# Ranking 32 experts by their number of rows and letting the ten smallest share TensorE in pairs

## The reference, cut to what matters

```python
gsel = jnp.argmax(lg, axis=-1)
le_sel = jnp.take_along_axis(le, gsel[:, None, None], axis=1)[:, 0]
top_p, top_i = lax.top_k(jax.nn.softmax(le_sel, axis=-1), TOP_K_INNER)
eid = gsel[:, None] * EXPERTS_PER_GROUP + top_i
hg = silu(einsum('nd,edf->nef', x, ewg)) * einsum('nd,edf->nef', x, ewu)
y = y + einsum('nef,efd->nd', hg * gate[:, sl, None], ewd)
```

## Time and profile before

| what | value |
|---|---|
| median of 3 runs | 1778.75 us (1776.92 to 1789.27) |
| the profiled execution | 1779.9 us |
| its span | 1778.1 us |
| TensorE busy | 1628.3 us (92%) |
| VectorE, ScalarE, GpSimd busy | 672.5, 434.6, 55.5 us |
| mean granted TensorE clock | 0.953 |
| moved by DMA | 246.90 MB |

### The profile page before, as it was taken

How to read it: one execution, slowest core, us unless ns; L and a number is a source line. 1 busy time by engine, 2 the same in 40 slices (tenths; PEclk the granted TensorE clock), 3 DMA queues, 4 the chain that set the end, 5 groups by cost and what they waited for, 6 DMA issues and landing times. The chain is left out here.

```text
span 1778.1 us, 34951 instructions
## 1 busy us (share of the span) xinstructions
PE 1628.3 (92%) x15296; PEld 1144.4 (64%) x15296; DVE 672.5 (38%) x1631; ACT 434.6 (24%) x891; POOL 55.5 (3%) x57
## 2 busy tenths in 40 slices
PE   7899989989988889998989879999999999995997
PEld 4566775775676656675757654555788888883443
DVE  5365464464364213415151442234411111112564
ACT  4413314214202202304131231112111111111344
POOL 0000000000000000000000000000100000002110
PEclk9898999998997889999999989999999999997999
DMA  5000001000010043403242472004799999976321
GB/s 183 27 27 12 15 17 38 13 16 13 15 41 20 3 195 129 169 27 155 119 179 119 186 276 97 36 36 158 273 368 368 366 371 368 365 297 221 111 83 42
DMA packets 57597, 246.90 MB, mean 139 GB/s; under 512 B 7520, under 2 KB 18016, under 8 KB 47712
## 3 DMA queue, kind: packets, MB, share of 16 engines
q1 hardware_dynamic: 45632, 201.61, 30.3%
q0 software_dynamic: 7200, 26.22, 4.1%
q10 hardware_dynamic: 4608, 16.78, 2.3%
HBM read 210.70 MB, written 33.88 MB: 138 GB/s over the span
## 5 line engine op out<-in xcount | busy, mean ns | idle before, releaser
L438 PE MATMUL bank<-h,w 128*128 128x352 f32 (+1 forms) x576 | 198.6, 495 | 6.4 <-DVE xb L997 6.4
L1750 PEld LDWEIGHTS bank<-cache,we 128*128 128x128 f32 x1536 | 175.1, 192 | 13.7 <-issue 10.5
L1750 PE MATMUL bank<-cache,we 128*128 128x128 f32 x1536 | 175.6, 275 | 2.8 <-DVE cache L2019 2.8
L438 PEld LDWEIGHTS bank<-h,w 128*128 128x128 f32 x576 | 109.7, 198 | 69.6 <-DVE xb L997 7.6
L2019 DVE COPY cache<-bank 128x512 f32<-128x512 f32 x64 | 41.3, 686 | 289.3 <-PE bank L1737 289.3
L1241 PE MATMUL bank<-h,w 128*128 128x352 f32 (+1 forms) x384 | 120.8, 477 | 5.5 <-POOL qd L1226 5.5
L1681 PE MATMUL bank<-cache,mixed 128*128 128x512 f32 x256 | 113.0, 600 | 6.4 <-DMA mixed<-in_pad_a 6.4
L2286 PE MATMUL bank<-we,unT 128*128 128x512 f32 x256 | 114.2, 604 | 1.4 <-DVE unT L2237 1.4
L1241 PEld LDWEIGHTS bank<-h,w 128*128 128x128 f32 x384 | 74.2, 194 | 50.4 <-POOL qd L1226 6.1
L1681 PEld LDWEIGHTS bank<-cache,mixed 128*128 128x128 f32 x256 | 48.7, 193 | 65.5 <-issue 58.9
L2286 PEld LDWEIGHTS bank<-we,unT 128*128 128x128 f32 x256 | 48.9, 194 | 60.4 <-issue 58.6
(11 more groups left out here) (405 smaller groups left out, 2499.2 us busy)
## 6 DMA issues: line engine op xcount, KB each, us to landing
we<-in_weg SPq DMA_DIRECT2D x24, 1024.0 KB, 5.3
we<-in_weu SPq DMA_DIRECT2D x24, 1024.0 KB, 8.6
we<-in_wed SPq DMA_DIRECT2D x24, 1024.0 KB, 11.2
cache<-in_kcj SPq DMA_DIRECT2D x4, 5120.0 KB, 15.7
cache<-in_vcj SPq DMA_DIRECT2D x4, 5120.0 KB, 15.1
y_rows<-cache ACTq DMA_DIRECT2D x32, 512.0 KB
cache<-in_weg SPq DMA_DIRECT2D x8, 1024.0 KB
cache<-in_weu SPq DMA_DIRECT2D x8, 1024.0 KB
```

What stands on the lines that cost most here:

```text
L438: mm = pe.matmul(out[:, 0:w], w3[:, KIND[q], kd, :], g.uT[:, kd, a:a + w], start=(kd == 0), stop=(kd == KD - 1))
L1750: mm = pe.matmul(bank[6 + e % 2][:, 128 * (2 * a + f):128 * (2 * a + f) + CAP], w[:, k, 128 * f:128 * f + 128], xT[e % 2][:, k, :], start= ...
```

## The change

Places stand for experts. VectorE ranks the experts by their count, largest first, with experts 0 to 3 fixed in ranks 0 to 3. Ranks 0 to 9 have room for 128 rows, 10 to 21 for 96, 22 to 31 for 64 (`CAPS`). The table of tokens is reordered by rank into `idx`, and `order` holds the expert of each rank; SyncE reads it into a register and loads the weights from there (`load_chosen`). The 32 ranks make 27 turns (`TURNS`): ranks 0 and 1 singly, and then five times four single ranks and one pair of the last ten: 2 to 5, (22, 23), 6 to 9, (24, 25), and so on to 18 to 21, (30, 31). Loads follow the order of the turns through the same four slots; a load waits for the `down` of the turn that had its slot.

In a pair, each expert has 64 rows. Both are gathered into one buffer and turned at once. In `up` the 64 columns of `xT` are the stationary side and 256 columns of the weights move, each expert in its half of the array; the result has rows by hidden columns, so after SiLU and product two transposes (`hidden_turn`) turn it for `down`, which again uses both halves. Rows are stored densely, 3072 in all. `rows` is split in `first_rows` (after turns 1 and 2) and `later_rows` (after turns 3 and 4), with each expert's own room and start. The later passes run if any expert has more rows than its rank has room for.

```diff
+CAPS = [128] * 10 + [96] * 12 + [64] * 10
+BASE = [sum(CAPS[:e]) for e in range(NE)]
+SINGLES, PAIRED = CAPS.index(64), list(range(CAPS.index(64), NE, 2))
+TURNS = [(e,) for e in range(SINGLES - 4 * len(PAIRED))]
+for n, e in enumerate(PAIRED):
+    TURNS += [(len(TURNS) - n + i,) for i in range(4)] + [(e, e + 1)]
+NU = len(TURNS)
+IN_TURN = [e for places in TURNS for e in places]
+load_of = {e: n for n, e in enumerate(IN_TURN)}
+turn_of = lambda e: next(u for u, places in enumerate(TURNS) if e in places)
+rows_in = lambda u: sum(CAPS[e] for e in TURNS[u])
+pairs_to = lambda u: sum(len(places) == 2 for places in TURNS[:u + 1])
+gathers_to = lambda u: sum(len(TURNS[n]) for n in range(u % NX, u + 1, NX))
...
+def load_chosen(sp, g, slot, e, loaded):
+    wg, wu, wd = slot
+    at = bass.ds(e, 1)
+    sp.dma_start(wg, g.d_weg[at].rearrange("o (p k) f -> p (o k) f", p=128)).then_inc(loaded, 16)
+    sp.dma_start(wu, g.d_weu[at].rearrange("o (p k) f -> p (o k) f", p=128)).then_inc(loaded, 16)
+    sp.dma_start(wd, g.d_wed[at].rearrange("o (f p) d -> p (o f) d", p=128)).then_inc(loaded, 16)
...
-        LOADS = ((gain, g.d_ffn_gain), (wr, g.d_wr), (br, g.d_br), (upper, g.d_upper), (iota, g.d_iota), (valid[:, :], g.d_valid),
-                 (w4, g.d_w4), (w32, g.d_w32), (tokv[:, :], g.d_tokv), (i32t, g.d_i32t), (pad_a, g.d_pad_a))
+        LOADS = ((gain, g.d_ffn_gain), (wr, g.d_wr), (br, g.d_br), (upper, g.d_upper), (iota, g.d_iota),
+                 (w4, g.d_w4), (w32, g.d_w32), (fixed, g.d_fixed), (i32t, g.d_i32t), (valid, g.d_valid), (tokv, g.d_tokv), (pad_a, g.d_pad_a))
...
-                sp.wait_ge(s["idx"], 1)
+                sp.wait_ge(s["ordered"], 2)
                 load_expert(sp, g, weights[3], 3, w_in[3])
-                for e in range(NW, NE):
-                    sp.wait_ge(s["down"], e - NW + 1)
-                    load_expert(sp, g, weights[e % NW], e, w_in[e % NW])
-                sp.wait_ge(s["down"], NE - 2)
+                for n in range(NW, NE):
+                    e = IN_TURN[n]
+                    which = sp.value_load(order[0:1, e:e + 1], min_val=0, max_val=NE - 1)
+                    sp.wait_ge(s["down"], turn_of(IN_TURN[n - NW]) + 1)
+                    load_chosen(sp, g, weights[n % NW], which, w_in[n % NW])
+                sp.wait_ge(s["down"], turn_of(IN_TURN[NE - 3]) + 1)
                 for k in range(KD):
...
-                for e in range(NE):
-                    if e >= NX:
-                        pool.wait_ge(s["x_turned"], e - NX + 1)
-                    pool.indirect_dma_start(xg[e % NX], None, g.xn[:, :], bass.IndirectOffsetOnAxis(idx[:, e:e + 1], 0)).then_inc(xg_in[e % NX], 16)
+                for u, places in enumerate(TURNS):
+                    if u >= NX:
+                        pool.wait_ge(s["x_turned"], u - NX + 1)
+                    for i, e in enumerate(places):
+                        pool.indirect_dma_start(xg[u % NX][64 * i:64 * i + CAPS[e], :], None, g.xn[:, :],
+                                                bass.IndirectOffsetOnAxis(idx[0:CAPS[e], e:e + 1], 0)).then_inc(xg_in[u % NX], 16)
...
+                def up(u):
+                    pe.wait_ge(s["xev"], u + 1)
+                    for e in TURNS[u]:
+                        pe.wait_ge(w_in[load_of[e] % NW], 48 * (load_of[e] // NW + 1))
+                    if u >= 2:
+                        pe.wait_ge(s["h"], u - 1)
+                    if len(TURNS[u]) == 2:
+                        for a in range(2):
                             for k in range(KD):
-                                mm = pe.matmul(bank[6 + e % 2][:, 128 * (2 * a + f):128 * (2 * a + f) + CAP], w[:, k, 128 * f:128 * f + 128],
-                                               xT[e % 2][:, k, :], start=(k == 0), stop=(k == KD - 1))
+                                for i, e in enumerate(TURNS[u]):
+                                    mm = pe.matmul(bank[6 + u % 2][64 * i:64 * i + 64, 256 * a:256 * a + 256], xT[u % 2][:, k, 64 * i:64 * i + 64],
+                                                   weights[load_of[e] % NW][a][:, k, :], start=(k == 0), stop=(k == KD - 1))
+                    else:
+                        (e,) = TURNS[u]
+                        for a in range(2):
+                            for f in range(2):
+                                for k in range(KD):
+                                    mm = pe.matmul(bank[6 + u % 2][:, 128 * (2 * a + f):128 * (2 * a + f) + CAPS[e]], weights[load_of[e] % NW][a][:, k, 128 * f:128 * f + 128],
+                                                   xT[u % 2][:, k, 0:CAPS[e]], start=(k == 0), stop=(k == KD - 1))
...
+                def hidden_turn(u):
+                    pe.wait_ge(s["gated"], pairs_to(u))
+                    for f in range(2):
+                        mm = pe.transpose(bank[6 + u % 2][:, 128 * f:128 * f + 128], sg_rows[u % 2][:, 128 * f:128 * f + 128], g.ident[:, :])
+                    mm.then_inc(s["h_turned"], 1)
...
                     for c in range(2):
                         for f in range(2):
-                            mm = pe.matmul(bank[2 * (e % 2) + c][:, :], hT[e % 2][:, f, :], weights[e % NW][2][:, f, 512 * c:512 * c + 512],
-                                           start=(f == 0), stop=(f == 1))
+                            for i, e in enumerate(TURNS[u]):
+                                mm = pe.matmul(bank[2 * (u % 2) + c][64 * i:64 * i + CAPS[e], :], hT[u % 2][:, f, 64 * i:64 * i + CAPS[e]],
+                                               weights[load_of[e] % NW][2][:, f, 512 * c:512 * c + 512], start=(f == 0), stop=(f == 1))
...
+                for u in range(NU):
+                    up(u)
+                    if u + 1 < NU:
+                        gather_turn(u + 1)
+                    if u >= 1:
+                        down(u - 1)
+                    if len(TURNS[u]) == 2:
+                        hidden_turn(u)
+                down(NU - 1)
...
-                op(dve.tensor_reduce(most, bank[5][:, 0:NE], AX.X, ALU.max))
-                dve.tensor_copy(g.most[:, :], most)
+                pairs = lambda x: x.unsqueeze(1).broadcast_to([128, NE, NE])
+                each = lambda x: x.unsqueeze(2).broadcast_to([128, NE, NE])
+                turns = place[0].rearrange("p t q -> p (t q)")[:, 0:NE * NE].rearrange("p (r e) -> p r e", r=NE)
+                op(dve.tensor_copy(counts, bank[5][:, 0:NE]))
+                op(dve.scalar_tensor_tensor(out=key, in0=counts, scalar=float(NE), in1=fixed, op0=ALU.mult, op1=ALU.add))
+                op(dve.tensor_tensor(chosen, pairs(key), each(key), ALU.is_gt))
+                op(dve.tensor_reduce(spot, chosen, AX.X, ALU.add))
+                op(dve.tensor_tensor(chosen, pairs(spot), each(i32t), ALU.is_equal))
                 dve.wait_ge(s["found"], 1)
-                dve.tensor_copy(idx[:, :], bank[7][:, 0:NE]).then_inc(s["idx"], 1)
+                op(dve.tensor_tensor(turns, pairs(bank[7][:, 0:NE]), chosen, ALU.mult))
+                op(dve.tensor_reduce(key, turns, AX.X, ALU.add))
+                dve.tensor_copy(idx[:, :], key).then_inc(s["idx"], 1)
+                dve.tensor_tensor(turns, pairs(i32t), chosen, ALU.mult)
+                dve.drain()
+                op(dve.tensor_reduce(key, turns, AX.X, ALU.add))
+                op(dve.tensor_scalar(cap, spot, float(CAPS.count(128)), 32.0, ALU.is_lt, ALU.mult))
+                dve.tensor_copy(order[:, :], key).then_inc(s["ordered"], 1)
+                dve.drain()
+                op(dve.tensor_scalar(key, spot, float(NE - CAPS.count(64)), 32.0, ALU.is_lt, ALU.mult))
+                op(dve.scalar_tensor_tensor(out=cap, in0=key, scalar=64.0, in1=cap, op0=ALU.add, op1=ALU.add))
+                dve.tensor_scalar(key, spot, float(NE - CAPS.count(64)), 32.0, ALU.min, ALU.mult)
+                dve.tensor_scalar(counted, spot, float(CAPS.count(128)), 32.0, ALU.min, ALU.mult)
+                dve.drain()
+                op(dve.scalar_tensor_tensor(out=spot, in0=spot, scalar=64.0, in1=key, op0=ALU.mult, op1=ALU.add))
+                op(dve.tensor_tensor(spot, spot, counted, ALU.add))
+                op(dve.tensor_tensor(key, counts, cap, ALU.subtract))
+                op(dve.tensor_reduce(most, key, AX.X, ALU.max))
+                op(dve.tensor_scalar(most, most, 0.0, None, ALU.max))
+                dve.tensor_copy(g.most[:, :], most).then_inc(s["ordered"], 1)
...
+                def of_expert(k, out, x):
+                    op(dve.tensor_tensor(v32[:, :, :], oh[k][:, :, :], bc(x, NE), ALU.mult))
+                    op(dve.tensor_reduce(out, v32[:, :, :], AX.X, ALU.add))
...
+                def later_rows(k):
+                    p, eid = position[:, k, :], pos
+                    of_expert(k, t1, cap)
+                    op(dve.tensor_tensor(over, p, t1, ALU.is_ge))
+                    op(dve.tensor_tensor(t1, t1, over, ALU.mult))
+                    op(dve.tensor_tensor(p, p, t1, ALU.subtract))
```

(50 more changed lines are left out.)

137 lines of the change are left out of this document (59 added, 78 removed).

## The result

The changed kernel takes 1792.45 us at the median (1786.14 to 1799.62), the kernel before 1780.67 us in the same comparison: a ratio of 1.0057, interval 1.0042 to 1.0073. By the ratio it is slower by about 10 us (7.5 to 13.0; the medians differ by 11.8), where 1769 was forecast and the range ended at 1792. The profiled execution took 1786.82 us around a span of 1785.0.

The account below looks back on a forecast made before the run. TensorE's period was taken to bound the expert stage, with DMA almost as full. A change of -12.4 us to the stage's end and +2.5 behind it gave -9.9: 1770.0 us profiled, 1769 us at the median, range 1746 to 1792.

Parts of the forecast that it names:

- What bounds the kernel: Expert stage: TensorE never waits and sets the period, 11.46 us per expert, with DMA almost as full at share 0.98.
- Routing, 96-row places, pairs, switches: Expert stage: no row overflows, 96 rows save PE nothing, a pair takes 12.0 us including 0.4 for width switches.
- The rival without sharing: Pairs' `up` and `down`: the two halves do not share the array, +10.4 us per pair, 1821 us; chance 0.04.
- DMA per six experts: Expert stage: six weight loads and the rows of five turns take DMA 61 us, against 57.8 for PE.
- The new wait: `up` of each pair but the first: TensorE waits 7 us for a chain of four loads taking 41.5 us.
- The clock: Behind each pair's 7 us wait: TensorE runs at half clock for a while, losing 1.8 us (bounds 0 and 3.5).
- The cycle of 65.0: Expert stage: four singles and a pair, from one pair's `up` to the next, take 65.0 us against 68.8 before.
- Ahead of the stage: Routing and first turns: ranking, half clock, an added constant, row numbers and a late load delay the first pair 8.4 us.
- Behind it: Hand-over after the expert stage: later-issued `pgate` loads share DMA with the last store and gathers, +2.5 us (0 to 5).
- the clock rival: Expert stage: 3.5 us of half clock per wait, a longer slow start, 5 us behind the stage; 1782 us, chance 0.12.
- Slower landing: Expert stage: loads of chosen experts land slower, each us per load adding 16; 1802 us at 10 us, chance 0.09.
- Full rate: Expert stage: DMA keeps its full rate when loads queue, 15.4 us less and waits of 3 us; 1750 us, chance 0.27.

Follow-up runs that it names:

- experiment 3: Changed kernel without transferring the down weights from the fifth load on, so its output is not the reference's; 1743.17 us, ratio 0.9778 to the kernel before.
- experiment 8: Changed kernel with gate and up weights requested after `up`, `later_rows` after turns 10 and 20, two spare singles last; 1737.38 us, ratio 0.9786.
- experiment 2: Kernel before the change, with gate and up weights requested after `up` and down weights after `down`; 1782.32 us, ratio 0.9998.
- experiment 4: Changed kernel with 32 single turns and no pairs; ranking, rooms and load order stay; 1795.83 us, ratio 1.007 to the kernel before.
- experiment 5: Changed kernel with `later_rows` run after turns 10 and 20 in place of 3 and 4; 1788.6 us, ratio 1.0047 to the kernel before.
- experiment 6: Changed kernel with products of constants into a free PSUM bank ahead of five waits for weights; 1781.04 us, ratio 1.0009 to the kernel before.

## Why the prediction was wrong, point by point

- **What bounds the kernel** held: experiment 3 removes traffic and PE is busy for 230 of 230 us; experiment 8 has both limits at once.
- **Routing, 96-row places, pairs, switches**: no later passes ran, which would have added some 2 ms; the rest is right, to 0.1 us in the 57.8 us of a cycle (57.9). The rival without sharing is dead.
- **DMA per six experts, 61 us**: right where the loads queue (61.3 and 61.0 in experiment 8).
- **The new wait** is the step that failed. It took only one dependence into account, the pair that needs two loads at once, and had all singles ready in time: "none of length at singles". The text listed the releases itself, two together at the end of `down(pair)`, but never compared each load's lead with the 11.75 us that it had worked out above. Four slots and turns that take one leave two periods of lead; a turn that takes two leaves one, 11.5. The load for `up` at 1355.75, at 1367.93 and at 1427.14 came 1.1, 0.5 and 0.8 us late, the one for 1442.89 4.05; in all eight such waits make 10.5 us, where nothing was charged.
- A second part of that step is the chain's length. From the pair's release (1354.83) to the fourth landing (1400.44) it took 45.6 us, where 41.5 was taken and 43 was the upper bound: the three gaps inside it are 10.9 us each, at a full share and 365 GB/s (the first window above). Part of it is a slip: the sum priced 3.3 turns' rows at 2.45 us, the price of 96 rows, but singles 6 to 9 have room for 128 (3.26), 2.7 us more. The third chain, with 96 rows, took 44.0. Hence 9.5 and 9.0 us at two pairs in place of 7. Where a single had waited long before, the pair's wait is 0.7 and 1.6: the delay moves to the earlier turn, it does not go.
- **The clock** had the right size at pairs, 1.8 us: 1.7, 2.3 and 1.6 at the first, second and fourth, nothing at the third and fifth. It was charged three times in the cycles and came at single places too, with 3.3 us at 1442.89 (10.41 us to the next turn for 7.12) and 3.0 at 1566.31 (10.15). The first cycle adds up: 57.8 of work, 1.7 of half clock, waits of 1.14, 0.48 and 9.52, in all 70.6 of 71.2. The second: 57.8 + 2.3 + 0.83 + 4.05 + 3.3 + 0.68 = 69.0 of 69.3.
- **The cycle of 65.0** follows from these. It was 69.0 on the mean. The four, with the clock and the lighter last chain, were forecast at 265.4 - 2.5 = 262.9 and took 276.0, which is 13.1 more. The parts, over four cycles: at the singles 10.5 us of waits and 6.3 of half clock, both forecast at nothing; at the pairs 20.8 of waits for 26.3, and 5.6 of half clock for 5.4; and 1.6 that is spread. So what was missed is the singles' 16.8 us; the pairs gave 5.3 of it back. From `rank` to the stage's end the forecast was -12.9 (-12.4 less the constant's 0.5), and +0.2 came (387.3 against 387.1): the 13.1 are the whole of the miss there.
- **Ahead of the stage**: from `rank` to `idx` 14.0 us where 10.56 were before, +3.4 (predicted 3.2). From `rank` to the first pair's `up` 96.2 where expert 6 had 86.3, +10.0 for a predicted 7.9 (8.4 less the constant's 0.5, which lies ahead of `rank`). Its parts are +3.9 up to the first `up` (3.4 taken), 2.65 of half clock in it (10.06 us in place of 7.41; 1.8 taken), and waits of 0.60 and 2.36 for the copies behind `later_rows` (2.4 taken); the rest, 0.4, is spread over the starts behind them. The last pair gave the 2.1 us back: 15.1 us from its `up` to the end for 17.2. The constant's 0.5 can't be seen: the wait for `in_pad_a` is 6.51 and 7.18 us at the weight loads of two kernels with the same code there (before and experiment 2), and 6.4 to 8.3 in those with the constant.
- **Behind it**: +4.5 us up to the first product for a predicted 2.5, in its bounds; 0.6 of it is made up by the end of the span.
- **The rivals**: the clock rival gave 1782 and is nearest in time. Its 10.5 us of half clock in the cycles is near the 11.9 measured, but it had them all at pairs, and it had no waits at singles. Slower landing is the right place for the wrong cause: a load alone takes 11.7 to 14.2 us to be whole, mostly near the 11.75 of before, and experiment 4 has no wait for a load, so addresses from registers are not what costs. Full rate never came for long.
- **What stays open**: R grew by 4.1 us, and the ratio says 10 (7.5 to 13.0). The stretch ahead of `rank` was 2.8 us longer in the one profiled execution; whether that is the kernel's or that execution's can't be told, as it varies by 14 us between executions.

## What to carry to other kernels

With a ring of slots, write down for each load when its slot is released and when it is needed, in periods, and hold that against the time from request to landing; a step that takes two slots halves the lead of all loads around it, not only its own. When merging steps shortens the compute, release each part of a slot at its last reader, and wait for each part at its first, before counting on the gain: here that turned +10 us into about -32, by the ratios. And where DMA stands at 0.98 beside a full PE, the gain from less compute ends at what the transfers need by themselves, here 61 us per six experts once the lead is used up, and not PE's 57.8.

## What was unexpected of the hardware

- Half clock follows short waits too, and not by their length alone. After 4.05 us idle the granted clock was 0.73 and then 0.80 in the windows around it, and `up` took 3.3 us longer. In experiment 5 the `up` at 1498.69 followed 2.08 us idle and took 10.5 us at a mean granted clock of 0.67; in experiment 8 the one at 1474.44 followed 3.37 us idle and took 7.1 at 1.00. Keeping TensorE at work on constants through most of the wait (experiment 6) kept the window 1330 to 1560 at 0.99 where it was 0.94.

```profile
1440.00:1446.00 6.00, 3.11 (x15) 3.14 (x15) 0.00 (x0) 0.00 (x0) 0.00 (x0) 0.73 1.02 347
1446.00:1455.00 9.00, 9.00 (x61) 8.51 (x61) 0.62 (x2) 0.33 (x1) 0.39 (x1) 0.80 1.02 417
```

- Of two loads requested 2.4 to 2.9 us apart, the second was whole after 21.2, 22.7, 20.5 and 17.8 us, the first after 13.0, 16.3, 12.0 and 12.6, where a load alone took 11.7 to 14.2. So the second waits for the first, and mostly the first is hardly held up.
- A single place of 64 rows costs PE 0.43 us more than one of 128 (11.89 against 11.46), spread over its `up`, turn and `down` with their changes of width.
